# Head stage of a hybrid decoder step: full-row tiles in place of 16- and 64-row ones

## The reference, cut to what matters

```python
logw = jnp.where(causal, b[..., :, None] - b[..., None, :] + ig[..., None, :], -jnp.inf)
inter = b + m[..., None]
m_t = jnp.maximum(inter, jnp.max(logw, axis=-1))
w_inter = jnp.exp(inter - m_t)
s = jnp.einsum('bhtd,bhsd->bhts', q, k) * jnp.exp(logw - m_t[..., None])
num = w_inter[..., None] * jnp.einsum('bhtd,bhde->bhte', q, C) + jnp.einsum('bhts,bhse->bhte', s, v)
den = w_inter * jnp.einsum('bhtd,bhd->bht', q, n) + jnp.sum(s, axis=-1)
h = num / jnp.maximum(jnp.abs(den), jnp.exp(-m_t))[..., None]
decay = jnp.exp(b[..., -1] + m - m_new)
wk = jnp.exp(b[..., -1:] - b + ig - m_new[..., None])
C_new = decay[..., None, None] * C + jnp.einsum('bhs,bhsd,bhse->bhde', wk, k, v)
n_new = decay[..., None] * n + jnp.einsum('bhs,bhsd->bhd', wk, k)
```

## Time and profile before

| | us |
|---|---|
| median of 3 runs | 1912.51 |
| span of the profiled execution, first to last instruction | 1911.0 |
| PE busy | 1889.9 (99%) |
| VectorE busy | 941.6 (49%) |
| ScalarE busy | 689.5 (36%) |
| GpSimd busy | 34.5 (2%) |

### The profile page before, as it was taken

One profiled execution on the slowest core, in us unless ns is written; L12 is line 12 of the kernel. 1 busy time (PEld: TensorE's weight loads), 2 busy tenths in 40 slices (PEclk: granted clock), 3 DMA queues, 4 the chain that ended last, 5 costly groups with the idle time before them and its releaser, 6 DMA issues.

```text
span 1911.0 us, 33610 instructions
## 1 busy us (share of the span) xinstructions
PE 1889.9 (99%) x12647; PEld 1855.8 (97%) x12647; DVE 941.6 (49%) x1045; ACT 689.5 (36%) x825; POOL 34.5 (2%) x67
## 2 busy tenths in 40 slices
PE   7999999999999999999999999999999999999998
PEld 7999898989899999999999999999999999999997
DVE  6565545454454444445555544455444544455544
ACT  5344343434343333333443333333333333333331
POOL 1001000010100000000000000000000000000000
PEclk9999999999999999999999999999999999999998
DMA  7446564756465545544454444444444444444442
GB/s 208 144 127 190 132 213 133 220 119 216 138 177 146 151 143 155 152 148 148 143 172 156 140 159 145 151 150 141 160 145 151 150 147 154 143 154 151 145 155 78
DMA packets 294469, 293.86 MB, mean 154 GB/s; under 512 B 12506, under 2 KB 292314, under 8 KB 294300
## 3 DMA queue, kind: packets, MB, share of 16 engines
q1 hardware_dynamic: 283464, 282.67, 48.8%
q10 hardware_dynamic: 10692, 9.51, 1.6%
q0 software_dynamic: 272, 1.12, 0.1%
HBM read 281.10 MB, written 12.17 MB: 153 GB/s over the span
## 4 chain that ended last, share of the span: by engine, by line
PE 98%; DVE 1%; DMA 0%; issue 0%; ACT 0%; SPq 0%; DVEq 0%; ACTq 0%
PE ps L1250 97%; DVE y_out L1243 0%; PE ps L1350 0%; DMA x_tok<-in_x_sample_dram 0%; PE ps L1270 0%; DVE x_low L840 0%; DVE x_T L843 0%; PE ps L1507 0%; DVE w_low L823 0%; ACT x_high L561 0%; PE ps L1451 0%; DVE sq_acc L1216 0%; DVE x_T L1212 0%; ACT tmp L790 0%; DVEq L110 0%
## 5 line engine op out<-in xcount | busy, mean ns | idle before, releaser
L823 DVE TENSOR_TENSOR w_low<-raw,w_high 128x1024 fp32r<-128x1024 f32 x512 | 621.7, 1226 | 609.0 <-ACT w_high L543 605.1
L543 ACT ACTIVATE w_high<-raw 128x1024 fp32r<-128x1024 f32 x512 | 534.9, 1055 | 712.5 <-PE ps L1250 709.1
L1250 PE MATMUL ps<-x_high,w_high 128*128 128x320 f32 (+2 forms) x2432 | 755.5, 311 | 1.3 <-PE ps L1250 1.1
L1250 PE MATMUL ps<-x_low,w_high 128*128 128x320 f32 (+2 forms) x2432 | 755.8, 311 | 0.0
L1250 PE MATMUL ps<-x_high,w_low 128*128 128x320 f32 (+2 forms) x2432 | 753.2, 310 | 0.0
L1250 PEld LDWEIGHTS ps<-x_high,w_high 128*128 128x128 f32 x2432 | 457.5, 188 | 7.2 <-issue 4.6
L1250 PEld LDWEIGHTS ps<-x_high,w_low 128*128 128x128 f32 x2432 | 458.6, 189 | 0.0
L1250 PEld LDWEIGHTS ps<-x_low,w_high 128*128 128x128 f32 x2432 | 457.3, 188 | 0.1
L1250 PE MATMUL ps<-u_high,w_high 128*128 128x320 f32 x1024 | 316.5, 309 | 0.0
L1250 PE MATMUL ps<-u_low,w_high 128*128 128x320 f32 x1024 | 316.4, 309 | 0.0
L1250 PE MATMUL ps<-u_high,w_low 128*128 128x320 f32 x1024 | 316.4, 309 | 0.0
(11 more groups left out here) (250 smaller groups left out, 1160.2 us busy)
## 6 DMA issues: line engine op xcount, KB each, us to landing
raw<-in_w_in_dram SPq DMA_DIRECT2D x176, 512.0 KB, 3.8
raw<-in_w_up_dram SPq DMA_DIRECT2D x128, 512.0 KB, 3.9
raw<-in_w_down_dram SPq DMA_DIRECT2D x128, 512.0 KB, 3.4
raw<-in_w_o_dram SPq DMA_DIRECT2D x32, 512.0 KB, 3.5
C_state<-in_state_mlstm_C_dram SPq DMA_DIRECT2D x16, 512.0 KB, 6.5
raw<-in_state_mlstm_C_dram SPq DMA_DIRECT2D x16, 512.0 KB, 4.1
out_dram<-C_state ACTq DMA_DIRECT2D x8, 1024.0 KB, 6.8
raw<-in_p_a_dram SPq DMA_DIRECT2D x16, 512.0 KB, 4.3
```

Of the source, the lines that this page charges most:

```text
L543: a.activation(wh[:, s % RING], raw[:, s % RING], ACT.Copy).then_inc(high_done, 1)
L823: v.tensor_tensor(wl[:, s % RING], raw[:, s % RING], wh[:, s % RING].bitcast(F32), ALU.subtract).then_inc(low_done, 1)
L1250: return pe.matmul(out, lhsT, rhs, start=start, stop=stop)
```

## The change

The last 16 prompt tokens and the 64 sample tokens form one tile of 80 (`KT`, `QT`), with a mask of its own (`tail_mask`), in scores, numerator and denominator. For the state updates those 80 tokens are cut into two groups of 40, and each group is stacked three times in 120 rows. VectorE and ScalarE fill the three parts of k and v so that one product of 120 rows gives high by high, low by high and high by low (`kw_stack`, `v_stack`). Each sequence then needs one product for each half of C instead of two; the mask buffers are two, with a third for the prompt's share of the stack. The prompt's state is made in fp32r from `kw_high`, `kw_low`, `v_high` and `v_low`: three products for each 128-token tile and one with the stack, 258 columns. The n update moves behind unit 23, as two products, with its VectorE operation and its store. `rows_split` and `chosen_head` grow from 36 to 128 rows, the added ones zero. v is transposed once more for the tile of 80. h uses the memory of `sq_acc`, and a gap tile goes. The constants on GpSimd follow the new shapes.

```diff
-    KT = [(0, P), (P, P), (2 * P, NMETA), (TP, TS)]
-    QT = [(T0, TP - T0, 0), (P, TP - P, TP - T0), (2 * P, TP - 2 * P, 2 * TP - T0 - P),
-          (TP, TS, 3 * TP - T0 - 3 * P)]
-    SW = QT[3][2] + TS
+    KT = [(0, P), (P, P), (2 * P, T - 2 * P)]
+    QT = [(T0, TP - T0, 0), (P, TP - P, TP - T0), (2 * P, T - 2 * P, 2 * TP - T0 - P)]
+    NR = T - 2 * P
+    SW = QT[2][2] + NR
+    SG = NR // 2
+    SK = 3 * SG
+    UG = SG // DS
+    PU = (TP - 2 * P) // DS
+    KR = 2
+    assert NR == 2 * SG and SK <= P and SG % DS == 0 and PU < UG and DS * (PU + NB) == NR
+    in_stack = [divmod(PU + b, UG) for b in range(NB)]
...
-        smask = tile(heads, "sample_mask", [TS, NB, DS])
-        onehot = tile(heads, "onehot", [2 * TS, NB], F32R)
+        tmask = tile(heads, "tail_mask", [NR, NR])
...
-            kwm = tile(st, "kw_masked", [2 * TS, NB // 2, DK], F32R)
-            kw = tile(st, "kw_tok", [P, 3, DK])
-            kws = tile(st, "kw_sample", [2 * TS, DK], F32R)
-            vt = tile(st, "v_tok", [P, 4, DV + 1])
-            vsh = tile(st, "v_sample_high", [2 * TS, DV], F32R)
-            vsl = tile(st, "v_sample_low", [TS, DV], F32R)
+            kwm = tile(st, "kw_masked", [SK, KR + 1, DK], F32R)
+            kwh = tile(st, "kw_high", [P, 2, DK], F32R)
+            kwl = tile(st, "kw_low", [P, 2, DK], F32R)
+            kst = tile(st, "kw_stack", [SK, 2, DK], F32R)
+            vt = tile(st, "v_tok", [P, 3, DV])
+            vth = tile(st, "v_high", [P, 2, DV + 2], F32R)
+            vtl = tile(st, "v_low", [P, 2, DV + 2], F32R)
+            vst = tile(st, "v_stack", [SK, 2, DV + 2], F32R)
...
-            kT = tile(st, "k_T", [P, GB, T + TS])
-            hT = tile(st, "h_T", [P, GB, TO])
+            kT = tile(st, "k_T", [P, GB, T + 2 * SK])
             cpo = tile(st, "C_prompt_out", [P, GB, DV + 1])
             nin = tile(st, "n_in", [NB, DK])
-            nso = tile(st, "n_sample_out", [NB, DK])
-            tile(st, "gap", [P, GAP])
...
+            nso = nin
             Cs = tile(st, "C_state", [P, NB, GB, DV])
             ha = tile(st, "h_a", [P, MW // P, TO])
         heads.close()
@@ -218,6 +231,7 @@
             mgl = tile(st, "merged_low", [P, KB, TO], F32R)
             clast = tile(st, "conv_last", [(TAPS - 1) * (1 + NB), CW])
...
-            g.memset(vt[:, :, DV:DV + 1], 1.0).then_inc(s_qmz, 1)
...
             g.memset(qm[:].bitcast(F32), 0.0).then_inc(s_qmz, 1)
             with pool.Fori(0, H) as h:
 
                 pool.wait_ge(s_kwl, h + 1)
                 pool.wait_ge(s_cup, 1 + 8 * h)
-                for b in range(NB):
-                    if b >= NB // 2:
-                        pool.wait_ge(s_cup, 1 + 8 * h + b - NB // 2 + 1)
-                    g.tensor_tensor(kwm[:, b % 4, :], kws[:].bitcast(F32), onehot[:, b:b + 1].bitcast(F32).to_broadcast([2 * TS, DK]),
-                                    ALU.mult).then_inc(s_kwm, 1)
+                g.tensor_tensor(kwm[:, KR, :], kst[:, 0, :].bitcast(F32), last_of[:, 0:1].to_broadcast([SK, DK]),
+                                ALU.mult).then_inc(s_kwm, 1)
+                for b, (group, at) in enumerate(in_stack):
+                    if b >= KR:
+                        pool.wait_ge(s_cup, 1 + 8 * h + b - KR + 1)
+                    g.tensor_tensor(kwm[:, b % KR, :], kst[:, group, :].bitcast(F32),
+                                    unit_of[:, at:at + 1].to_broadcast([SK, DK]), ALU.mult).then_inc(s_kwm, 1)
             pool.wait_ge(s_clo, 1)
...
                         if out.shape[2] > T:
-                            ins = a.activation(out[:, b, T:], tmp[:, b, TP:T], func,
+                            ins = a.activation(out[:, b, T:].rearrange("p (g r t) -> p g r t", r=3, t=SG),
+                                               three_times(tmp[:, b, 2 * P:T]), func,
...
-                        for n, (k0, nk) in enumerate(KT[0:3]):
-                            a.activation(kw[0:nk, n, :], M[n // 2][0:nk, (n % 2) * DK:(n % 2 + 1) * DK],
-                                         ACT.Copy, scale=wkcol[0:nk, n, ds(h, 1)])
-                        a.activation(kws[:], M[1][:, DK:2 * DK], ACT.Copy,
-                                     scale=wkcol[:, 3, ds(h, 1)]).then_inc(s_kw, 1)
+                        act.wait_ge(s_nso, 1 + h)
+                        for n in range(2):
+                            a.activation(kwh[:, n, :], M[0][:, DK * n:DK * n + DK], ACT.Copy,
+                                         scale=wkcol[:, n, ds(h, 1)])
+                        for n in range(2):
+                            ins = a.activation(kst[:, n, :], M[1][0:SK, DK * n:DK * n + DK], ACT.Copy,
+                                               scale=wklow[:, n, ds(h, 1)])
+                        ins.then_inc(s_kw, 1)
                     if p == 11:
                         act.wait_ge(s_sc, h + 1)
                         add_bias(2, kT, BV)
                     if p == 13:
                         act.wait_ge(s_vtr, h + 1)
-                        for n, (k0, nk) in enumerate(KT):
-                            a.activation(vt[0:nk, n, 0:DV], M[n // 2][0:nk, (n % 2) * DV:(n % 2 + 1) * DV], ACT.Copy)
-                        a.activation(vsh[:], M[1][:, DV:2 * DV], ACT.Copy).then_inc(s_vt, 1)
+                        by_tile = M[0][:].rearrange("p (n e) -> p n e", n=2)
+                        a.activation(vth[:, :, 0:DV], by_tile, ACT.Copy)
+                        a.activation(vst[:, :, 0:DV], M[1][0:SK, :].rearrange("p (n e) -> p n e", n=2), ACT.Copy,
+                                     scale=part_of[:, 1:2]).then_inc(s_vt, 1)
+                        a.activation(vt[:, 0:2, :], by_tile, ACT.Copy)
+                        a.activation(vt[0:NR, 2, :], M[3][0:NR, 0:DV], ACT.Copy).then_inc(s_vt, 1)
...
-                        act.wait_ge(s_nso, 1 + h + 1)
-                        act.dma_start(n_sample[0, :, ds(h, 1), :].rearrange("b o d -> b (o d)"), nso[:]) \
-                            .then_inc(s_out, 16)
...
                         add_bias(4, tmp[:, :, 0:TO], BO, ACT.Sigmoid)
+                        act.wait_ge(s_nso, 1 + h + 1)
+                        act.dma_start(n_sample[0, :, ds(h, 1), :].rearrange("b o d -> b (o d)"), nso[:]) \
+                            .then_inc(s_out, 16)
...
-                row(ins)
+                row(v.tensor_tensor(samp(wkr), samp(arw), mx[:, :, DS - 1:DS].to_broadcast([H, NB, DS]), ALU.subtract))
+                row(v.tensor_copy(wkr[:, T:].rearrange("p (g r t) -> p g r t", r=3, t=SG), three_times(wkr[:, 2 * P:T])))
...
                         dve.wait_ge(s_pick, 4)
                         dve.wait_ge(s_const, 3)
                         dve.wait_ge(s_bcp, 1 + h)
-                        v.tensor_scalar(chosen[:], ones[0:32 + H, :], pick[:, ds(h, 1)], None,
+                        v.tensor_scalar(chosen[:], ones[:], pick[:, ds(h, 1)], None,
                                         ALU.mult).then_inc(s_chosen, 1)
...
-                        up = slice(TS, 2 * TS)
-                        v.scalar_tensor_tensor(kws[up, :], M[1][up, DK:2 * DK], wkcol[up, 3, ds(h, 1)],
-                                               kws[up, :].bitcast(F32), ALU.mult, ALU.subtract).then_inc(s_kwl, 1)
+                        for n in range(2):
+                            v.scalar_tensor_tensor(kwl[:, n, :], M[0][:, DK * n:DK * n + DK], wkcol[:, n, ds(h, 1)],
+                                                   kwh[:, n, :].bitcast(F32), ALU.mult, ALU.subtract)
+                        for n in range(2):
+                            ins = v.scalar_tensor_tensor(kst[:, n, :], M[1][0:SK, DK * n:DK * n + DK],
+                                                         wkcol[0:SK, 2 + n, ds(h, 1)], kst[:, n, :].bitcast(F32),
+                                                         ALU.mult, ALU.subtract)
+                        ins.then_inc(s_kwl, 1)
...
-                        dve.wait_ge(s_vt, h + 1)
-                        v.tensor_tensor(vsl[:], M[1][0:TS, DV:2 * DV], vsh[0:TS, :].bitcast(F32),
-                                        ALU.subtract).then_inc(s_vsl, 1)
-                        dve.wait_ge(s_np, h + 1)
-                        dve.wait_ge(s_nin, 16 * h + 16)
-                        dve.wait_ge(s_out, 16 + 48 * h)
-                        v.scalar_tensor_tensor(nso[:], nin[:], deccol[:, ds(h, 1)], M[3][0:NB, 0:DK],
-                                               ALU.mult, ALU.add).then_inc(s_nso, 1)
+                        dve.wait_ge(s_vt, 2 * h + 1)
+                        v.tensor_tensor(vst[:, :, 0:DV], M[1][0:SK, :].rearrange("p (n e) -> p n e", n=2),
+                                        vst[:, :, 0:DV].bitcast(F32), ALU.subtract)
+                        dve.wait_ge(s_vt, 2 * h + 2)
+                        v.tensor_tensor(vtl[:, :, 0:DV], M[0][:].rearrange("p (n e) -> p n e", n=2),
+                                        vth[:, :, 0:DV].bitcast(F32), ALU.subtract).then_inc(s_vsl, 1)
...
```

(65 more changed lines are left out.)

92 lines of the change are left out of this document (59 added, 33 removed).

## The result

The changed kernel takes 1864.69 us (median of 4 runs, 1864.11 to 1865.84), the kernel before on the same chip 1912.3 us (4 runs, 1911.69 to 1912.95): a ratio of 0.9751, 95% interval 0.9739 to 0.9763. Forecast were 1865 us, 1860 to 1880. A second measurement, on another chip, gave 1864.82 against 1911.97 us, 0.9753 (0.9739 to 0.9766). The span of the profiled execution fell from 1911.0 to 1862.4 us.

A forecast was written before the change was run, and what follows sets the result against it. TensorE, busy 99% of the span, was taken as the bound; gains of 12.1 us per head, 48.5 for four, less 0.8, gave a span of 1863.3 us. With 1.5 us from span to median: 1865 us, range 1860 to 1880.

The forecast's parts named there:

- Rival A: Whole kernel: the sum of the gains on PE holds, 1861 to 1869 us; chance 0.62.
- F: The products are not issued as the code reads and little is gained, 1900 to 1912 us; chance 0.04.
- state updates: Units 19 to 22: eight products a unit become four on 120 rows at 0.12 us each; gain 8.1 us a head.
- numerator, denominator: Behind unit 18: 5.51 us become 3.65 with a tile of 80; gain 1.85 us a head.
- prompt state: Behind the denominator: twelve fp32 records become 14 products at 0.12 us, 3.43 to 1.68 us; gain 1.75 a head.
- scores: The 16- and 64-column parts become four records of 80 columns, 0.28 us; gain 0.4 us a head.
- row broadcast: Behind unit 2: 36 rows become 128, so 0.71 us become 0.33; gain 0.38 us a head.
- added products and transposes: Two more transposes, and the n product twice behind unit 23 in place of once; loss 0.34 us a head.
- B: 120 rows are another mode than 128, costing time at group borders: 1873 us, or 1879 if partial tiles never overlap loads; chance 0.16.
- D: Weight loads do not overlap between products on the same rows, so each costs 0.30 us: 1887 us; chance 0.03.
- C: Another engine becomes late at units 15 to 18 or in front of h: 1869 to 1873 us; chance 0.12.
- The end of the stage: After the last head PE waits for n_sample before transposing z_last: 0.8 us lost, once.

The follow-up runs named there:

- number 1: The kernel before, with the second product of each state update on 128 rows instead of 64, the added rows zero: 1887.0 us, ratio 0.9871.
- number 2: The changed kernel with the state-update products cut from 120 to 64 rows: 1870.84 us.
- number 4: The changed kernel with the third key tile of numerator and denominator cut from 80 to 64 rows: 1868.63 us.
- number 6: The changed kernel with the row broadcast behind unit 2 cut back from 128 to 36 rows: 1865.69 us.
- Number 8: The changed kernel with GpSimd's zeroing of q_masked made to wait until VectorE has made the first head's chosen_head: 1863.54 us.
- number 9: The changed kernel again, unaltered, for comparing small differences on the same chip: 1864.82 us.
- number 3: The changed kernel with the state-update products cut from 120 to 72 rows: 1864.81 us.

## Why the prediction was right

Rival A, that the sum holds, is what happened: 1864.7 for 1865. F falls too: the products stand in the timeline as the code reads. Term by term, in us a head, from the distances of units in the two traces:

| step | forecast | measured |
|---|---|---|
| state updates | 8.1 | 8.1 |
| numerator, denominator | 1.85 | 1.99 |
| prompt state | 1.75 | 1.66 |
| scores | 0.4 | 0.44 |
| row broadcast | 0.38 | 0.36 |
| added products and transposes | -0.34 | -0.4 |
| sum (99.80 less 87.65) | 12.1 | 12.15 |

*The rows.* The Trainium skill ("TensorEngine Tiling (Array Packing)", Key Properties) says that a change of tiling mode drains TensorE. The traces agree in so far as time is lost at each change, and the runs add the rest: 72, 80 and 120 rows go as 128, and a change costs 0.18 to 0.20 us (numbers 1, 2, 4 and 6). B falls by the group at 305.20, where 120 rows cost nothing at either border.

*Loads.* D falls: products on the same rows stand 0.12 us apart with a load of 0.188 us each, here with 120 rows as before with 128. The Trainium skill ("TensorE: Matmul & The Clock Gate", The mechanism) lists loads as overlapping only matmuls of another row group, which would have these one behind the other; the same section also names a background weight buffer that would allow the overlap. The trace shows the overlap and not what makes it possible.

*Short fp32 records.* A pair of 80 columns costs 0.18 us, not the 0.22 that I took from half of the excess of two small pairs; number 4 shows why for most of it: of the 0.64 us of excess two changes of kind make 0.35, and 80 rows have none. The rest would be a third change, from 16 to 64 rows, which no run took by itself. This is the 0.14 that the block gained over the forecast.

*Slack.* Unit 17's low half is 1.09 us ahead of PE, unit 18's 1.36 (forecast 0.7 to 1.3). h is ready at 212.49 and wanted behind unit 19 at 213.54: 1.05 (forecast 1.0). ScalarE stood idle for 2.68 us ahead of its first high half of h_a (to 500.43); by its code the landing of n_sample is the likely cause, though the profile names none, and PE's list of waits has no entry for it. C, as put, did not happen.

*The end of the stage.* 0.94 us idle for 0.8, and 1.1 by the distance of units (from unit 23 of head 3 to merge's first 4.41 us before, 5.65 after, of which 0.13 belong to every head).

*What was wrong.* One step costed at nothing was not nothing: "GpSimd, 2% busy, builds some ten more small constants, long before they are read." One of them is built right before the first head and pushed a memset, and with it VectorE's chosen_head, 1.1 us later: PE stood idle for 0.78 us, unit 2 took 4.86 us in place of 3.83, and head 0 gained 11.25 us in place of 12.15. Number 8, which takes the memset out of the way, brings unit 2 back to 3.83 us. I had looked at who reads the constants, not at what they delay on their own engine and beside it.

*How it came out to 0.3 us nevertheless.* The stage from head 0 to head 3 lost 46.6 us: 4 x 12.15 = 48.6, less 1.1 at its end, less 0.9 in head 0. Forecast were 47.7. In the two profiled executions the start (up to unit 0 of head 0) is 1.2 us and the tail (from the start of the last unit) 0.7 us shorter besides; number 9, the same kernel, has 0.4 and 0.7. Everything between the head stage and the last unit takes the same 1348.03 us in both. The medians differ by 47.6 and 47.15. So 0.5 to 1 us of the agreement is start and tail, and that is chance: the start has been seen to vary by 1.5 us, and the tail is 19.8 us in number 1 as well, which but for the rows is the kernel before.

## What to carry to other kernels

Where TensorE is the bound, look at the number of rows of each stationary tile before its columns or its format: a group of products on 64 rows or fewer between full ones cost two changes of some 0.19 us here (36 and 64 rows were tried), and alternating tiles paid at every step; padding with zeros to more than 64 rows cost PE nothing (numbers 1 and 3). Keep like with like, and price a row by the start of the next, since the loss shows behind the small tile too (0.42 for 0.31 us).
An operation on a nearly idle GpSimd is not free: ask what stands behind it in its queue, and which VectorE operation runs beside it.

## What the runs showed of the hardware that was not expected

- Padding 64 rows to 128 with zeros, with the number of products and their columns as before, took 24.5 us off a kernel of 1911.5.
- 72 rows behave like 128, 64 do not (1864.81 and 1870.84 us).
- A VectorE operation of 0.28 us lasted 2.08 us beside a GpSimd memset of 1.92 us and ended with it. The Trainium skill ("SBUF — State Buffer", SBUF: two separate sides) describes the pair of ports that the two engines share as an exclusive lock held for a whole instruction, taken by whichever starts first; the trace agrees in that the ends are 0.09 us apart. It does not show the memset to be first: the record of the VectorE operation starts 0.07 us ahead of it (150.27 and 150.34).
- A wait of PE for its own last product costs 0.57 us, twice the idle time that the list of waits shows for it.
